# Reordering the page sums, the gate products and the output weights in a hybrid attention and mixture-of-experts decoder step

## The reference, cut to what matters

```python
h = rmsnorm(x, g_pre_mix) * (1 + sc1) + sh1
qa, ka, va, qb, kb, vb, logf, ga, gb = mixer_inputs(h, w_in, b_f, pos)     # ga, gb: sigmoid gates
# fox_sample: scores of 8 new rows against 2048 past keys that lie in pages of 128
c_past = cumsum(logf_past, axis=1)                 # running sums over all 16 pages of a sequence
s_past = q @ k_past / sqrt(64) + cq - c_past       # the "past bias"
# merge_branches
mix = (ga * (oa @ w_pa) + gb * (ob @ w_pb)) @ w_o
x = x + gt1 * rmsnorm(mix, g_post_mix)
h2 = rmsnorm(x, g_pre_ffn) * (1 + sc2) + sh2       # then a router and 32 experts, two for each row
```

## Time and profile before

| what | us |
|---|---|
| median of 3 runs | 1142.53 |
| fastest, slowest | 1139.91, 1147.29 |
| the profiled execution's own time | 1148.97 |
| span of its instructions | 1147.0 |
| TensorE busy | 989.9 (86%) |
| VectorE, ScalarE, GpSimd busy | 380.7, 205.8, 186.9 |
| mean granted TensorE clock | 0.934 of full |

### The profile page before, as it was taken

One profiled execution on the slowest core, in us unless ns is written; L12 is line 12 of the kernel. 1 busy time (PEld: TensorE's weight loads), 2 busy tenths in 40 slices (PEclk: granted clock), 3 DMA queues, 4 the chain that ended last, 5 costly groups with the idle time before them and its releaser, 6 DMA issues.

```text
span 1147.0 us, 17923 instructions
## 1 busy us (share of the span) xinstructions
PE 989.9 (86%) x7324; PEld 582.4 (51%) x7324; DVE 380.7 (33%) x877; ACT 205.8 (18%) x509; POOL 186.9 (16%) x210
## 2 busy tenths in 40 slices
PE   3999999998999699699999898699959997777770
PEld 2444444444466366476667564364545554444430
DVE  3200033215864364483057313103631230011005
ACT  3000000003445111002100212102411111111114
POOL 0000043302210103131221111000022332222110
PEclk9999999999899699799999899699959999999995
DMA  9997766787769599899999785996279999999956
GB/s 322 364 317 271 255 248 238 257 277 256 249 224 312 181 300 334 311 363 342 360 326 347 297 293 195 370 336 285 100 311 357 367 372 389 377 387 395 412 239 247
DMA packets 96845, 349.32 MB, mean 305 GB/s; under 512 B 11674, under 2 KB 55458, under 8 KB 77438
## 3 DMA queue, kind: packets, MB, share of 16 engines
q1 hardware_dynamic: 79262, 266.75, 64.8%
q0 software_dynamic: 15552, 79.97, 19.0%
q10 hardware_dynamic: 1952, 1.48, 0.5%
HBM read 336.31 MB, written 63.36 MB: 348 GB/s over the span
## 4 chain that ended last, share of the span: by engine, by line
PE 36%; DMA 21%; DVE 4%; SPq 2%; issue 1%; ACT 1%; ACTq 0%; DVEq 0%; POOLq 0%
DMA w_all<-in_w_exp 15%; PE bank L1632 10%; PE bank L2222 5%; PE bank L2050 4%; PE bank L1570 3%; PE bank L1508 2%; PE bank L1624 2%; PE bank L2070 2%; DVE mods L1736 1%; PE bank L1622 1%; DMA turned<-in_w_o 1%; PE bank L1493 1%; SPq L2121 1%; DMA c_pages<-w_all 1%; DMA bias<-c_pages 1%
## 5 line engine op out<-in xcount | busy, mean ns | idle before, releaser
L1632 PE MATMUL bank<-turned,w_all 128*128 128x320 f32 (+1 forms) x512 | 143.9, 425 | 3.7 <-ACT w_all L1680 3.7
L459 PE MATMUL bank<-w_all,turned 128*128 128x481 f32 (+2 forms) x384 | 119.3, 503 | 1.1 <-DVE turned L668 1.1
L459 PE MATMUL bank<-w_ring,turned 128*128 128x481 f32 (+2 forms) x384 | 118.4, 502 | 0.0
L2050 PE MATMUL bank<-w_all,mix_row 128*64 128x256 f32 x736 | 94.0, 413 | 28.3 <-DMA w_all<-in_w_exp 27.3
L1632 PEld LDWEIGHTS bank<-turned,w_all 128*128 128x128 f32 x512 | 94.4, 194 | 38.9 <-issue 18.7
L2050 PEld LDWEIGHTS bank<-w_all,mix_row 128*64 128x64 f32 x736 | 61.8, 150 | 67.5 <-issue 47.7
L1736 DVE STREAM_TRANSPOSE mods<-w_all 128x2048 f32<-128x2048 f32 (+1 forms) x39 | 86.3, 2238 | 6.6 <-DMA w_all<-in_cache_b_k,key_rows 3.2
L459 PEld LDWEIGHTS bank<-w_all,turned 128*128 128x128 f32 (+1 forms) x384 | 56.9, 172 | 61.5 <-issue 58.3
L459 PEld LDWEIGHTS bank<-w_ring,turned 128*128 128x128 f32 (+1 forms) x384 | 57.2, 172 | 60.3 <-issue 57.3
L2096 DVE COPY act_t<-bank 128x128 f32<-128x128 f32 x33 | 9.6, 292 | 199.7 <-PE bank L2060 198.0
L678 DVE COPY w_all<-bank 128x481 f32 (+5 forms) x32 | 16.9, 531 | 152.6 <-PE bank L459 152.4
(11 more groups left out here) (357 smaller groups left out, 1293.4 us busy)
## 6 DMA issues: line engine op xcount, KB each, us to landing
w_all<-in_w_exp SPq DMA_DIRECT2D x22, 2048.0 KB, 40.1
out_a_sample<-in_cache_a SPq DMA_DIRECT2D x8, 4080.0 KB, 21.4
w_all<-in_w_exp SPq DMA_DIRECT2D x25, 1024.0 KB, 37.8
mods<-in_w_ada SPq DMA_DIRECT2D x21, 1024.0 KB, 7.1
w_all<-in_cache_a SPq DMA_DIRECT2D x22, 512.0 KB, 7.2
turned<-in_w_exp SPq DMA_DIRECT2D x5, 2048.0 KB, 42.2
mods<-in_w_exp SPq DMA_DIRECT2D x5, 2048.0 KB, 43.5
w_all<-in_cache_a SPq DMA_DIRECT2D x36, 256.0 KB, 6.0
```

What stands on the lines that cost most here:

```text
L459: mm = nc.tensor.matmul(m.banks[i][r:r + ROWS[i], 0:hi - lo], m.hT[:, k, i * P:i * P + ROWS[i]], ring[u][:, CW * k + lo:CW * k + hi], star ...
L1632: mm = nc.tensor.matmul(GATE[:, 0:WIDTH[h]], gate_w[b][k][:, c % 2 * P:(c % 2 + 1) * P], m.hT[:, k, 256 * h:256 * h + WIDTH[h]], start=k = ...
L2050: mm = nc.tensor.matmul(m.banks[2 + p][x * SLOTS:(x + 1) * SLOTS, 0:HID], hgT[:, k, :], m.weights(u)[:, (2 * k + x) * HID:(2 * k + x + 1) ...
```

## The change

Six edits, all in the order of work; no arithmetic is added.

- `running_sums` moves from step 6 to step 3; `totals` and with it `past_sums` from after step 7 to after step 5; `scaled_terms` from step 12 to step 6. `SUMS` becomes 5, the write to DRAM is at SUMS + 2 (step 7, before 10), the read back at SUMS + 3 (step 8, before 12), the sort at step 12 (before 14), the write of the sorted sums at step 13 (before 15), the first bias loads at step 14 (before 16).
- All bias loads but the first four go from SP's queue to ScalarE's.
- END is 78 instead of 82: the last of the 80 pieces is in step 77.
- SP issues w_o at step 80, `(3, "k", 6)`, ahead of the loads of the last unit's values, and no longer waits for `v_num[N - 7]`; w_pa and w_pb are issued after the loop, when the value step 88 is done.
- The first tile's products with w_o, `mix(0, 0)` and `mix(0, 1)`, are done in phase c in four parts of four instructions, after value steps 86 to 89, and are gone from phase d.
- ScalarE's wait for its own last copy is gone from its end.

```diff
+        m.wo_pe = ctx.enter_context(nc.semaphore("w_o_sums"))
...
         if part == "k":
+            if (u, g) == (0, 5):
+                use(t, "after", "totals", u, 0)
...
-            if (u, g) == (0, 0):
-                use(t, "after", "totals", u, 0)
...
-    SUMS = at[(0, "v", 0)]
+    SUMS = at[(0, "v", 0)] - 2
...
-    FIRST, END = 1, 82
+    FIRST, END = 1, 78
...
+            def output_weights():
+                sp.wait_ge(mixed, 2 * KD)
+                sp.wait_ge(gate_pe, len(sums))
+                sp.wait_ge(v_used, max(v_num[n] for n in v_num if slot_of[n] in (1, 2, 3)) + 1)
+                sp.wait_ge(turned, len(k_num))
...
+                sp.dma_start(by_slot[:, 0:3, :], w_o[:, 0:3, :]).then_inc(m.wo_in, 16)
+                sp.dma_start(by_slot[:, 3:slots, :], w_o[:, 3:slots, :]).then_inc(m.wo_in, 16)
...
+                sp.dma_start(rest, w_o[:, slots:KD, :]).then_inc(m.wo_in, 16)
...
             for t in range(N):
                 n = t + KV_RING - 1
+                if t == at[(3, "k", 6)]:
+                    output_weights()
...
-                for u in (1, 2):
-                    first = at[(u, "k", 0)]
-                    for x in range(4):
-                        if t == (at[(u, "k", 4 * (x - 1) + 1)] if x >= 2 else SUMS + 9 if u == 1 else first - 4):
-                            past_bias(u, x)
+                if t == SUMS + 9:
+                    for x in range(2):
+                        first_bias(1, x)
...
-                if t == SUMS + 5:
+                if t == SUMS + 3:
                     sp.wait_ge(terms, 3)
...
+            sp.wait_ge(v_used, len(v_num) - 3)
             sp.dma_start(m.slot(0)[:, 0:2 * D], I["w_pa"]).then_inc(m.wp_in, 16)
...
+            def mix_first(h, k0):
+                pe.wait_ge(moved, KD)
+                pe.wait_ge(m.wo_in, 48)
+                for k in range(k0, k0 + 4):
+                    mm = nc.tensor.matmul((GATE, BOTH)[h][:, :], m.hT[:, k, 0:P], w_o[k][:, 512 * h:512 * (h + 1)], start=k == 0, stop=k == KD - 1)
+                if k0 == 4:
+                    mm.then_inc(m.wo_pe, 1)
+
+            mix_at = {at[(3, "v", 1 + x)]: divmod(x, 2) for x in range(4)}
...
+                if t in mix_at:
+                    h, x = mix_at[t]
+                    mix_first(h, 4 * x)
...
+            def past_bias(u, x):
+                act.wait_ge(s_out, chunk_at[(u, x - 2) if x >= 2 else (u - 1, x + 2)] + 1)
+                for h in range(2):
...
+                    act.dma_start(bias[:, b, :], src.unsqueeze(1).to_broadcast([16, DEC, 512])).then_inc(bias_in[b], 16)
+
+            bias_at = {at[(u, "k", 4 * (x - 1) + 1)]: (u, x) for u in (1, 2) for x in (2, 3)}
+            bias_at.update({at[(1, "k", 13)]: (2, 0), at[(2, "k", 2)]: (2, 1)})
...
-                if t == SUMS + 3:
+                if t == SUMS + 2:
                     act.wait_ge(pre, BH + 4)
...
+                    if (u, part, g) == (0, "k", 3):
+                        running_sums()
                     if (u, part, g) == (0, "k", 6):
-                        running_sums()
                         rows_of_pages()
+                        scaled_terms()
...
             pe.wait_ge(wo_in, 16 * 3)
-            for h in range(2):
-                mix(0, h)
             pe.wait_ge(wp_in, 32)
```

More of the change, by code:

```diff
@@ L1384, in merge_weights, with first_bias @@
                 merge_weights_in(sp, I, m, p)
-            def past_bias(u, x):
-                if (own(u), x) == (0, 0):
+            def output_weights():
[3 more added lines that the diff above has]
+                sp.wait_ge(turned, len(k_num))
+                w_o = I["w_o"].rearrange("p (k n) -> p k n", n=D)
+                slots = EXPERT_W // D
+                by_slot = m.slot(1).rearrange("p (k n) -> p k n", n=D)
+                sp.dma_start(by_slot[:, 0:3, :], w_o[:, 0:3, :]).then_inc(m.wo_in, 16)
+                sp.dma_start(by_slot[:, 3:slots, :], w_o[:, 3:slots, :]).then_inc(m.wo_in, 16)
+                rest = m.turned[:, KD * NT:KD * NT + (KD - slots) * D].rearrange("p (k n) -> p k n", n=D)
+                sp.dma_start(rest, w_o[:, slots:KD, :]).then_inc(m.wo_in, 16)
+            def first_bias(u, x):
+                if x == 0:
                     sp.wait_ge(ccum_out, 16)
-                if x >= 2:
-                    sp.wait_ge(s_out, chunk_at[(u, x - 2)] + 1)
-                elif own(u):
-                    sp.wait_ge(s_out, chunk_at[(u - 1, x + 2)] + 1)
                 for h in range(2):
@@ L1430, in _ @@
                     sp.dma_start(ccum.rearrange("u h s k -> (u h s) k"), rows_s).then_inc(ccum_out, 16)
-            sp.wait_ge(mixed, 2 * KD)
-            sp.wait_ge(gate_pe, len(sums))
-            sp.wait_ge(v_used, max(v_num[n] for n in v_num if slot_of[n] in (1, 2, 3)) + 1)
-            sp.wait_ge(turned, len(k_num))
-            w_o = I["w_o"].rearrange("p (k n) -> p k n", n=D)
-            slots = EXPERT_W // D
-            by_slot = m.slot(1).rearrange("p (k n) -> p k n", n=D)
-            sp.wait_ge(v_used, v_num[N - 7] + 1)
-            sp.dma_start(by_slot[:, 0:3, :], w_o[:, 0:3, :]).then_inc(m.wo_in, 16)
-            sp.dma_start(by_slot[:, 3:slots, :], w_o[:, 3:slots, :]).then_inc(m.wo_in, 16)
-            rest = m.turned[:, KD * NT:KD * NT + (KD - slots) * D].rearrange("p (k n) -> p k n", n=D)
-            sp.dma_start(rest, w_o[:, slots:KD, :]).then_inc(m.wo_in, 16)
+            sp.wait_ge(v_used, len(v_num) - 3)
             sp.dma_start(m.slot(0)[:, 0:2 * D], I["w_pa"]).then_inc(m.wp_in, 16)
@@ L1635, in piece @@
                     mm.then_inc(gate_pe, 1)
+            w_o = [*(m.slot(1)[:, k * D:(k + 1) * D] for k in range(EXPERT_W // D)),
+                   *(m.turned[:, KD * NT + k * D:KD * NT + (k + 1) * D] for k in range(KD - EXPERT_W // D))]
+            def mix_first(h, k0):
[6 more added lines that the diff above has]
+            mix_at = {at[(3, "v", 1 + x)]: divmod(x, 2) for x in range(4)}
             use_pe = {"probs": probs, "shares": shares, "fold": fold, "totals": totals}
@@ L1690, in exps @@
                     nc.scalar.activation(rows, rows, ACT.Exp, bias=nm[:, h:h + 1], accum_out=dn[:, h, 0:1]).then_inc(ex, 1)
+            def past_bias(u, x):
+                act.wait_ge(s_out, chunk_at[(u, x - 2) if x >= 2 else (u - 1, x + 2)] + 1)
+                for h in range(2):
+                    src = ccum[own(u), 4 * h:4 * h + 4, :, 512 * x:512 * (x + 1)].rearrange("h s k -> (h s) k")
+                    b = 2 * (x % 2) + h
+                    act.dma_start(bias[:, b, :], src.unsqueeze(1).to_broadcast([16, DEC, 512])).then_inc(bias_in[b], 16)
+            bias_at = {at[(u, "k", 4 * (x - 1) + 1)]: (u, x) for u in (1, 2) for x in (2, 3)}
+            bias_at.update({at[(1, "k", 13)]: (2, 0), at[(2, "k", 2)]: (2, 1)})
             nc.scalar.preload_act_table_set("exp_and_others")
             for t in range(N + 1):
+                if t in bias_at:
+                    past_bias(*bias_at[t])
                 for x in piece_at.get(t, []):
@@ L1893, in _ @@
                 if t < N:
-                    if (u, part, g) == (0, "v", 5):
-                        scaled_terms()
                     if part == "v" and g + 1 == COUNT[u]:
@@ L1976, in phase_d @@
         y_pe, y_out, mixed = [sem(n) for n in ("merge", "merge_read", "mixed")]
-        wo_pe, rs, wo_out, x_ok, h_ok = [sem(n) for n in ("w_o_sums", "rstd", "w_o_read", "residual", "h2")]
+        wo_pe = m.wo_pe
+        rs, wo_out, x_ok, h_ok = [sem(n) for n in ("rstd", "w_o_read", "residual", "h2")]
         t_pe, t_d, t_a, lg_pe, lg_out, filled = [sem(n) for n in ("turned", "t_dve", "t_act", "logits", "logits_out", "filled")]
```

1 line of the change is left out of this document (removed).

## The result

Slower, where faster was forecast. The changed kernel's median is 1159.44 us (4 runs, 1151.51 to 1163.08), beside 1144.78 for the kernel before (4 runs); the ratio is 1.0117, 95% interval 1.008 to 1.0155. The profiled executions take 1160.43 us (span 1158.6) and 1148.97 us (span 1147.0): 11.6 us more span.

The account below looks back on a forecast made before the run. Bound: expert loads at full DMA rate, starting once TensorE finishes phases c and d. Samples' products 18.9 us sooner, less 3.8 and 2.5, give 12.6 us; from median 1142.53 to 1129.9 us, range 1119 to 1140.

Parts of the forecast that it names:

- Page sums: Phase c: sums started sooner remove TensorE's 9.95 us wait for the first bias and keys; 11.6 us saved, bounds 0 and 13.
- I take back 2 us for loads that come late; bounds 0 and 8: Phase c before step 78: sooner steps need sooner loads while DMA shares are nine tenths or more; 2 us charged.
- Gate pieces sooner: Phase c, unit 2's exponentials: with END 78 the 3.70 us wait and most half clock behind it go; 5.5 us saved, bounds 0 and 6.
- Bias loads: Phase c: moving them to ScalarE's queue saves only issue time; nothing taken, bounds -3 and +2.
- Output weights: End of phase c: w_o issued near 693.5, last gather issued near 696.5 and used at 706, data up to step 86 at about 714.
- the third rival: Last values of phase c: w_o delays window values some 6 us, moved products run at lower clock; 1149.7 us, chance 0.07.
- Phase c ends at 742.8: End of phase c: against 742.6 before, page and tanh savings being spent on mix(0, h); bounds 737 and 757.
- +7.8: Phase c, steps 78 to 80: three pieces leave for earlier steps, which is no work saved; 7.8 us added back before step 78.
- A new wait of 3.8 us before L2259, and some 2.5 us of half clock after it: Phase d: TensorE finishes its products before the first tile is ready at start + 28.5; bounds for the two 0 and 12.
- The second: Front of phase c: 8 of 17.1 us saved come back as waits on loads or ScalarE's order; 1137.9 us, chance 0.19.

## Why the prediction was wrong

*Page sums, -11.6 us.* The mechanism was right. The first write came 33.8 us after phase c's start, where 33.0 was forecast (426.3 less 393.3). From it to the first bias's use it took 43.8 us and not 39.9, so the use at 466.68 meets the forecast 466.2 only because phase c had begun 4.2 us sooner, and 3.36 us of the wait are left. With whole rows the gain is there: the scoring of unit 1's new keys at 109.1 us after phase c's start against 120.7, and 8 to 12 us in the medians of three groups. That the first pair differs by just the forecast 11.6 us is luck: the same event lies at 117.6 and 124.5 in two other traces without the sooner sums. What failed is what I charged beside it.

*"I take back 2 us for loads that come late; bounds 0 and 8".* This is the step that failed. Both numbers were guesses from the DMA share, nine tenths or more in the stretch, and a share does not tell whose packets are moved. I should have asked which loads had got through because the pause of 9.95 us held the gathers back. The trace before held the answer: SP's weight loads right behind the pause landed in 6 to 8 us, with 0.6 us of issue. The pause removed, they took 29 to 42 us. Mending these loads alone takes the whole from 1.0117 to 0.9998, that is 1.2%, about 14 us (8 to 20, from the two intervals), where I had charged 2 and allowed 8.

*Gate pieces sooner, -5.5 us.* The wait went as forecast. The loads of these pieces were counted for their amount and not for their place: the step said "sooner steps need sooner loads" and did not ask what they are moved past on SP's queue. It was the last window keys: 6.2 us at once, 8.1 us in the part alone (3.4 before), +0.7% against the forecast -0.5%. With the order mended the step is worth nothing that can be measured (1.0011), so its -5.5 us was not there either.

*Bias loads, 0.* 0.9966 alone, 3.9 us (0.6 to 7.2) and so at the edge of its bounds; nothing with whole rows.

*Output weights.* The forecast has the last gather issued at 696.5 and used at 706, 9.5 us later and 6.4 us after the value steps in front of it, and gives this wait no line of its own. It took 11.2 us from issue to use and TensorE waited 8.34 us, against 3.78 before. The trace bore out the part of the third rival by which w_o slows what is beside it. Its other part, half clock for the moved products, did not come: they ran at 0.46 us each (3.70 us for eight), at full clock. W_o itself was issued at 711.57, 18 us behind the forecast 693.5, all of it lateness from before.

*Phase c ends at 742.8.* It ended at 760.57. With whole rows and END at 82 and the w_o part in place it ends 2.1 us later than before, in us after phase c's start (351.4 against 349.3), on the forecast's scale at 744.7. But this kernel lacks the shifted pieces, for which the forecast has -5.5, +7.8 and +2 us; without them it would say 738.5. So even with the loads mended this part is some 6 us short, in single traces, and which of its terms is too small stays open.

*Phase d.* "A new wait of 3.8 us before L2259, and some 2.5 us of half clock after it": the wait did not come, since TensorE needed 20.1 us instead of 10.7 for the samples' products. This step failed too. I took the saved 16.04 us of mix(0, h) as work and missed that the clock had come back during this run of wide products, ahead of the narrow ones, although I used the same observation (16.04 against 13.79 us) against the third rival. With the products left in place the samples' products are at full clock again.

*The rivals.* The second, "the front's gain is not there", has the gain come back as waits and names the right mechanism. Its 8 us were too few, as was its assumption that nothing is lost beyond the gain: the front was 17.0 us later at the last unit's first value step. The third gave the right sign and the wrong place.

## What to carry to other kernels

Before a long wait of the busiest engine is removed, list the transfers that were issued or landed within it or just behind it, on which queue, and in packets of what size: the pause may be what holds their rival queue back. The DMA share does not say it; the packet counts of the queues do. A load that must live beside large gathers should have wide rows; here that turned an edit worth nothing into one worth 0.8 to 1.1%. And a block of products during which the clock comes back can be worth its own time to the ones that follow, so moving it is not free even where its new place is.

The version that beats both kernels is the kernel before with the page sums two steps sooner and the gate and merge weights in whole rows: 1131.24 us, 0.9923 (0.9898 to 0.9948); with the bias on ScalarE's queue it is the same.

## What the runs showed of the chip

- *Two queues take turns by the packet.* With work on both, GpSimd's gathers and SP's loads moved 965 and 965 packets in 24 us of the changed kernel, and 778 and 779 in 20 us with whole rows. So a queue's bytes follow its packet size: 0.95 MB of 1 KB packets beside 7.01 MB, 2.19 MB of 2.8 KB packets beside 5.66 MB.
- *Row size under load.* A 512 KB load in rows of 1 KB, beside page gathers: 5.3 to 6.5 us of SP's time to issue and 37 to 42 us to land; in whole rows 0.43 us and 20 to 22 us. Where the gathers' queue ran dry, the narrow one took 0.61 and 7.5 us, with the DMA engines busy all the while. So the price of narrow rows shows only beside another queue's large packets. Why the issue itself is slow was not tried.
- *A busy TensorE can stay at the lower clock.* The samples' fp32 products of 64 columns, back to back, stayed at a granted clock of 0.50 for 19 us, the level of 1.2 GHz (421 ns each in the run with the w_o part); behind the products of 512 columns the same ones ran at 275 ns, in the kernel before and in the run with tile 1's first. What in these products makes the difference was not tried.
- *Single traces differ.* TensorE's waits for transposed page keys add up to 9.1 to 14.4 us in the six traces of kernels whose page sums were not moved, so only medians over several runs tell parts of half a per cent apart.
